# A paged-attention decoder step on one core: page numbers looked up once a turn by the sync engine

## The chip, the cores and the metric

The kernel runs on one core of a Trainium2 chip. The metric is the device time of one execution in microseconds (us); the median of several executions counts. Engines are called by their profile names: PE (TensorE matmul), PEld (its weight load), DVE (VectorE), ACT (ScalarE), POOL (GpSimd), SP (SyncE, which here only waits, looks up numbers and issues DMAs; its sequencer is SPq).

## What is computed

One step of a two-layer hybrid decoder. Layer A is a gated short convolution, layer B is forgetting attention with 16 heads of 64 over a shared set of keys and values, for 512 prompt tokens and for 8 sample sequences of 8 new tokens each. Each sample has 2048 past positions in 16 pages of 128 rows; which physical page holds which logical page stands in `page_table`:

```python
k_past = cache_k[page_table].reshape(nb, -1, N_HEADS, HEAD_DIM)
v_past = cache_v[page_table].reshape(nb, -1, N_HEADS, HEAD_DIM)
lf_past = cache_logf[page_table].reshape(nb, -1, N_HEADS).astype(jnp.float32)
k_all = jnp.concatenate([k_past, k_s.astype(k_past.dtype)], axis=1)
v_all = jnp.concatenate([v_past, v_s.astype(v_past.dtype)], axis=1)
F_all = jnp.cumsum(jnp.concatenate([lf_past, lf_s], axis=1), axis=1)
...
hs = _fox_layer(hs, sample_attend, b_norm[j], b_w_in[j], q_norm[j], b_w_out[j])
```

## The kernel before

It is written by hand: each engine has its own program, and semaphores join them. The order on an engine is the order of the code. Layer A and its output take the first 290 us. Then the queries of all heads are projected, and from about 377 us on there are eight turns (`heads(i)` on each engine, a hardware loop of seven turns and an unrolled last one).

Turn i does two things at once. It attends prompt head pair i, and it attends the past of sample i, for all 16 heads. The past needs 16 key pages and 16 value pages of 128 x 1024 numbers, 0.52 MB each. They pass through `page_ring`, 16 slots of 0.52 MB, which serves the keys first and the values after:

- Key slot n is loaded by two DMAs of 128 x 512 (0.26 MB, rows of 2 KB): slots 0 to 7 hold the first half of the heads' columns of all 16 pages, two pages a slot, slots 8 to 15 the second half. So each half looks up all 16 page numbers.
- DVE transposes each slot in place (line 1067), slots 0 to 3 at the end of the turn before, 4 to 7 and 8 to 15 in the turn itself.
- PE scores a half of the heads once eight slots are turned (`past_scores`, line 1450, 128 matmuls). Ahead of each half stands the last weight piece of a projection (line 1293), and PE waits in front of that piece for the eight transposes (`b_turned`).
- When half r is scored (`b_scored`), the value pages 8r to 8r + 7 may be loaded into its slots, one DMA of 128 x 1024 each (line 396).
- PE multiplies probabilities and values page by page (line 1557) between the prompt's steps; each step frees its slot (`b_used`), and the slot takes a key pair of the next sample.

SP issues nearly all DMAs in one queue. Its turn, in order: the prompt's log-forget sums (line 453), a weight slice of 0.52 MB (line 376), eight value pages, a weight slice, eight value pages, then the 16 key slots of the next sample, each behind `b_used`, with the suffix sums (1.05 MB, line 370) behind slot 8 and a weight slice behind slot 13, and the loop's branch (line 487). The other transfers of a turn are three stores of new keys and values, 0.56 MB, from ACT.

The page number comes from `page_of` (line 379): SP reads it from the SBUF tile `page_row` into a register, with a bounds check. Before each key slot there are two such lookups, before each value page one:

Of the kernel before, what the change touches and what calls it, by code (L numbers as in the profile page):

```python
# [31 lines left out]
P = 128  # L32
D = 1024
KT = D // P
SEQ = 512
NB = 8
NQ = 8
NS = NB * NQ
# [5 lines left out]
NPG = 16  # L44
# [3 lines left out]
NT = 5  # L48
# [4 lines left out]
HALF_D = D // 2  # L53
# [5 lines left out]
C_ID, C_ONESB, C_TRI, C_CM, C_NM, C_QD, C_RST, C_ONE = 0, 128, 256, 384, 512, 1024, 1088, 1152  # L59
# [18 lines left out]
def rows(t):  # L78
    return P if t < QB else NS
# [34 lines left out]
def build(nc, ctx, x_prompt, x_sample, state_conv, cache_k, cache_v, cache_logf, page_table,  # L114
# [9 lines left out]
    h_dram = nc.dram_tensor("h_scratch", [NT * P, D], F32, kind="Internal").ap()  # L124
# [4 lines left out]
    def place(name, shape, dt=F32, over=None):  # L129
        n = 4 if dt is not BF16 else 2  # L130
        for s in shape[1:]:
            n *= s
        n += (-n) % 32
        off = at["top"] if over is None else over
        if over is None:
            at["top"] += n
        at[name] = off
        return nc.alloc_sbuf_tensor_at(name, shape, dt, offset=off)
# [49 lines left out]
    def slot(n):  # L188
        return at["page_ring"] + n * 4 * D
# [5 lines left out]
    X2 = place("residual_b", [P, NT, D], over=slot(0))  # L195
# [27 lines left out]
    NBI = place("new_bias", [P, NB, NS], over=at["new_keys"] + 4 * NB * NS)  # L223
# [8 lines left out]
    def sem(name):  # L232
        return ctx.enter_context(nc.semaphore(name))
# [28 lines left out]
    b_used, b_qc, b_qt = sem("v_page_used"), sem("q_current_ready"), sem("q_pair_ready")  # L262
    b_turned, b_scored, b_taken = sem("k_pages_turned"), sem("past_scored"), sem("past_scores_taken")
    b_raw = [sem(f"b_w_loaded{s}") for s in range(2)]
    b_scaled, b_high, b_split, b_proj = sem("b_w_scaled"), sem("b_w_high"), sem("b_w_split"), sem("b_projected")
    b_dact, b_ddve = sem("proj_out_act"), sem("proj_out_dve")
    b_t0, b_t0f, b_t1, b_t1f = sem("turn0_full"), sem("turn0_free"), sem("turn1_full"), sem("turn1_free")
    b_c0, b_c0f, b_c1, b_c1f = sem("score0_full"), sem("score0_free"), sem("score1_full"), sem("score1_free")
    b_ss, b_ln, b_rr, b_normed = sem("head_squares"), sem("head_ln"), sem("head_rsqrt"), sem("head_normed")
    b_sfx, b_qz, b_nm = sem("suffix_loaded"), sem("q_spread_ready"), sem("new_mask_loaded")  # L270
# [13 lines left out]
    s_hld = sem("h_loaded")  # L284
# [9 lines left out]
    wo_b = b_w_out[0].rearrange("(k p) n -> p k n", p=P)  # L294
    kpages = cache_k.rearrange("g p h d -> g p (h d)")
    vpages = cache_v.rearrange("g p h d -> g p (h d)")
# [16 lines left out]
    def _(sp):  # L313
# [39 lines left out]
        def load_slab(w, col):  # L353
            sp.dma_start(WRA, w[:, :, bass.ds(col, SLAB)]).then_inc(l_raw, 16)
# [13 lines left out]
        def load_suffix(b):  # L368
            src = suffix_dram[bass.ds(b, 1), :, :].rearrange("a h n -> (a h) n")
            sp.dma_start(SS[:, :], src.unsqueeze(1).to_broadcast([H, NQ, PAST])).then_inc(b_sfx, 16)  # L370
# [4 lines left out]
        def load_w(w, col, slot):  # L375
            sp.dma_start(WR[:, slot, :, :], w[:, :, bass.ds(col, P)]).then_inc(b_raw[slot], 16)

        def page_of(b, n):
            return sp.value_load(PTAB[0:1, bass.ds(b * NPG + n, 1)], min_val=0, max_val=n_pool - 1)  # L379

        def load_keys(b, n, free=None):

            pages = [page_of(b, 2 * (n % 8) + e) for e in range(2)]
            if free:
                sp.wait_ge(*free)
            for e in range(2):
                src = kpages[bass.ds(pages[e], 1), :, n // 8 * HALF_D:(n // 8 + 1) * HALF_D]
                sp.dma_start(ring[:, n, e * HALF_D:(e + 1) * HALF_D],  # L388
                             src.rearrange("a p n -> (a p) n")).then_inc(b_page[n], 16)

        def load_values(b, n, free=None):
            page = page_of(b, n)
            if free:
                sp.wait_ge(*free)
            src = vpages[bass.ds(page, 1), :, :]
            sp.dma_start(ring[:, n, :], src.rearrange("a p n -> (a p) n")).then_inc(b_page[n], 16)  # L396

        sp.wait_ge(l_split, NSLAB)
# [4 lines left out]


        sp.wait_ge(s_rows, 16 * 9)
        sp.wait_ge(s_cs, H)
        for n in range(2):
            load_keys(0, n)
        for t in range(NT):
            sp.wait_ge(l_evac, 5 * (NSLAB - 1) + t + 1)  # L410
            sp.dma_start(h_dram[t * P:t * P + rows(t), :], X[0:rows(t), t, :]).then_inc(s_hst, 16)
        for n in range(2, 7):
            load_keys(0, n)
        sp.wait_ge(s_co, 1)
        sp.dma_start(conv_prompt[0, 0], CO[0:2, :]).then_inc(s_cost, 16)
        sp.dma_start(conv_sample[0].rearrange("b s n -> (b s) n"), CO[2:18, :]).then_inc(s_cost, 16)
# [3 lines left out]
        sp.wait_ge(s_hst, 16 * NT)  # L420
        sp.wait_ge(s_xl, 2 * NT)
        for n in range(7, 9):
            load_keys(0, n)

        sp.wait_ge(s_ft, 1)
        sp.dma_start(f_dram, FT[:, :]).then_inc(s_fst, 16)
# [5 lines left out]
        for n in range(4, KT + 3):  # L432
            sp.wait_ge(b_split, n - 1 if n < KT + 2 else n)
            if n < KT:
                load_w(wqz, n * P, n % 2)
            else:
                load_w(*((wkv, D), (wkv, 0), (wqz, KT * P))[n - KT], (0, 1, 1)[n - KT])
            if n < KT + 1:
                load_keys(0, 5 + n)
            if n == KT:  # L440

                sp.wait_ge(b_proj, 2)
                load_keys(0, 14)
                load_keys(0, 15)
        sp.wait_ge(s_fnr, 1)
        sp.dma_start(logf_prompt[0].rearrange("(t p) h -> p t h", p=P), LFN[:, 0:QB, :]).then_inc(s_out, 16)
        sp.dma_start(logf_sample.rearrange("b q h -> (b q) h"), LFN[0:NS, QB, :]).then_inc(s_out, 16)

        def heads(i, last):
            sp.wait_ge(b_c0f, 4 * i)  # L450
            sp.wait_ge(b_c1f, 4 * i)
            src = f_dram[bass.ds(2 * i, 2), 0:SEQ].unsqueeze(0).to_broadcast([P, 2, SEQ])
            sp.dma_start(FB[:, :, :], src).then_inc(b_fb, 16)
            if not last:
                sp.wait_ge(b_split, KT + 3 * i + 1)
                load_w(wkv, (i + 1 + KT) * P, 0)

            for n in range(NPG):
                load_values(i, n, (b_scored, 2 * i + n // 8 + 1) if n % 8 == 0 else None)
                if n == 7 and not last:  # L460
                    sp.wait_ge(b_split, KT + 3 * i + 3)
                    load_w(wkv, (i + 1) * P, 1)
            if last:
                sp.wait_ge(b_split, KT + 3 * NB)
                load_slab(wo_b, 0)

            for n in range(NPG):
                if last:
                    if n < NT:
                        sp.wait_ge(b_used, NPG * i + n + 1)  # L470
                        sp.dma_start(X2[0:rows(n), n, :], h_dram[n * P:n * P + rows(n), :]).then_inc(s_hld, 16)
                else:
                    load_keys(i + 1, n, (b_used, NPG * i + n + 1))
                if n == 8:

                    sp.wait_ge(b_t0, 8 * i + 4)
                    sp.wait_ge(b_t1, 8 * i + 4)
                    if last:
                        sp.dma_start(NBI[:, :, :].rearrange("p b n -> p (b n)"),
                                     table[:, C_NM:C_NM + NB * NS]).then_inc(b_nm, 16)  # L480
                    else:
                        load_suffix(i + 1)
                if n == 13 and not last:
                    sp.wait_ge(b_split, KT + 3 * i + 5)
                    load_w(wqz, (i + 1 + KT) * P, 1)

        with sp.Fori(0, NB - 1) as i:
            heads(i, False)
        heads(NB - 1, True)


        sp.wait_ge(b_t1f, 8 * NB)
# [1187 lines left out]
```

## Time and profile before

| | us |
|---|---|
| runs shown | 969.38, 959.49, 965.42; median 965.42 |
| profiled execution | 968.43 |
| its span | 966.6 |
| PE busy | 852.6 (88%) |
| DVE busy | 557.5 (58%) |
| ACT busy | 342.4 (35%) |
| POOL busy | 217.2 (22%) |
| mean DMA rate | 214 GB/s |

The profiled execution's own time is 1.8 us above its span. SP has no busy time in the profile, since it only issues; its instructions stand in the timeline and in the chain of work as SPq. Two ways of reading matter here. The timeline gives start and duration of merged instructions, and in brackets the idle time before them and what ended it. The chain in order of time lists pieces one after another; "issue" is time in which the engine waited for nothing that the profile shows.

### The profile page before, as it was taken

How to read it: one execution, taken by the hardware profiler on the slowest of the kernel's cores; microseconds unless marked ns; L12 is line 12 of the kernel's file. 1: busy time of each engine (PE TensorE's matmuls, PEld its weight loads, DVE VectorE, ACT ScalarE, POOL GpSimd, SP SyncE). 2: the span in 40 equal slices, each digit the busy share in tenths (PEclk: the TensorE clock that was granted, in tenths of full speed). 3: DMA queues.
4: the chain of work that ended last, by engine and by line, in shares of the span. 5: the costliest groups of instructions: out<-in, count | busy, mean ns of one | idle time of the engine just before them, and what ended most of it. 6: DMA issues, size and time to landing. Idle time of an engine off the chain costs nothing.

```text
span 966.6 us, 23640 instructions
## 1 busy us (share of the span) xinstructions
PE 852.6 (88%) x8516; PEld 707.5 (73%) x8516; DVE 557.5 (58%) x1039; ACT 342.4 (35%) x728; POOL 217.2 (22%) x130
## 2 busy tenths in 40 slices
PE   3899999999998997988787888887888878877998
PEld 2899999999997996756555656565556555654998
DVE  4745655555336355568485584684856746836632
ACT  4233333333025444252451442524514415235210
POOL 2233333331211032221322213203222132121000
PEclk8899999999999999899998998998999989989999
DMA  6232233323536463688998988998989889896212
GB/s 202 67 87 70 82 87 87 87 84 93 163 90 230 145 195 92 214 313 270 325 334 244 399 292 304 378 275 317 331 256 401 282 282 387 277 357 223 89 44 99
DMA packets 148482, 206.65 MB, mean 214 GB/s; under 512 B 10527, under 2 KB 93136, under 8 KB 147266
## 3 DMA queue, kind: packets, MB, share of 16 engines
q1 hardware_dynamic: 138802, 199.40, 61.6%
q10 hardware_dynamic: 9088, 4.46, 1.5%
q0 software_dynamic: 528, 2.10, 0.8%
q8 instruction: 20, 0.33, 0.1%
q14 instruction: 44, 0.36, 0.1%
HBM read 195.29 MB, written 10.63 MB: 213 GB/s over the span
## 4 chain that ended last, share of the span: by engine, by line
PE 54%; SPq 24%; issue 10%; DVE 7%; DMA 4%; ACT 1%; POOL 0%; DVEq 0%; ACTq 0%; POOLq 0%
PE psum L1293 31%; SPq L379 11%; PE psum L1319 9%; SPq L388 8%; PE psum L1450 4%; PE psum L1263 3%; SPq L396 2%; PE psum L1557 2%; DMA page_ring<-in_cache_k 2%; DVE page_ring L1067 1%; DMA w_raw<-in_a_w_in 1%; DMA w_raw<-in_a_w_out 1%; PE psum L1490 1%; PE psum L1512 1%; PE psum L1367 1%
## 5 line engine op out<-in xcount | busy, mean ns | idle before, releaser
L1293 PE MATMUL psum<-xn_high,w_high 128*128 128x256 f32 x992 | 230.4, 314 | 45.2 <-DVE page_ring L1067 42.3
L1293 PEld LDWEIGHTS psum<-xn_high,w_high 128*128 128x128 f32 x992 | 167.8, 193 | 79.3 <-DVE page_ring L1067 45.8
L1293 PE MATMUL psum<-xn_low,w_high 128*128 128x256 f32 x992 | 216.0, 300 | 0.0
L1293 PE MATMUL psum<-xn_high,w_low 128*128 128x256 f32 x992 | 215.5, 299 | 0.0
L1067 DVE STREAM_TRANSPOSE page_ring<-page_ring 128x1024 f32<-128x1024 f32 x128 | 153.4, 1224 | 32.8 <-DMA page_ring<-in_cache_k 31.2
L1293 PEld LDWEIGHTS psum<-xn_low,w_high 128*128 128x128 f32 x992 | 170.5, 193 | 0.0
L1293 PEld LDWEIGHTS psum<-xn_high,w_low 128*128 128x128 f32 x992 | 170.4, 193 | 0.0
L551 POOL TENSOR_TENSOR w_raw<-w_raw,gains 128x1024 f32<-128x1024 f32 x32 | 61.6, 1927 | 275.3 <-DMA w_raw<-in_b_w_in 244.0
L913 DVE TENSOR_TENSOR w_low<-w_raw,w_high 128x1024 fp32r<-128x1024 f32 x32 | 54.1, 1692 | 74.5 <-ACT w_high L629 74.5
L1450 PE MATMUL psum<-page_ring,q_current 32*32 32x512 f32 x2048 | 84.1, 700 | 0.0
L528 POOL TENSOR_TENSOR w_raw<-w_raw,gains 128x1024 f32<-128x1024 f32 x30 | 60.8, 2027 | 89.6 <-DMA w_raw<-in_a_w_in 89.6
L560 POOL TENSOR_TENSOR w_low<-w_raw,w_high 128x1024 fp32r<-128x1024 f32 x22 | 52.1, 2368 | 124.4 <-ACT w_high L680 124.4
L1557 PE MATMUL psum<-page_ring,p_turned 128*32 128x256 f32 x1024 | 75.2, 388 | 0.0
L629 ACT ACTIVATE w_high<-w_raw 128x1024 fp32r<-128x1024 f32 x32 | 33.9, 1060 | 94.8 <-PE psum L1293 67.7
L680 ACT ACTIVATE w_high<-w_raw 128x1024 fp32r<-128x1024 f32 x30 | 31.7, 1055 | 90.2 <-POOL w_raw L551 81.2
L1450 PEld LDWEIGHTS psum<-page_ring,q_current 32*32 32x32 f32 x2048 | 36.9, 112 | 36.0 <-issue 28.6
L1095 DVE COPY ks_t<-k_t 128x64 f32 (+1 forms) x8 | 2.2, 271 | 63.3 <-PE psum L1450 63.3
L1557 PEld LDWEIGHTS psum<-page_ring,p_turned 128*32 128x32 f32 x1024 | 23.4, 108 | 20.8 <-issue 13.6
L731 ACT ACTIVATE q_current<-queries 32x64 f32 (+1 forms) x128 | 32.5, 254 | 3.9 <-DVE queries L1044 1.0
L1080 DVE COPY probs_t<-psum 128x512 f32<-128x512 f32 (+3 forms) x32 | 15.4, 482 | 26.6 <-PE psum L1263 26.4
L796 ACT ACTIVATE probs<-probs,tiny 128x512 f32<-128x512 f32 (+1 forms) x32 | 19.3, 605 | 24.5 <-DVE tiny L1129 23.4
L1263 PE MATMUL psum<-constants,sample_scores 128*128 128x128 f32 x128 | 18.6, 278 | 10.6 <-DVE p_turned L1080 8.6
(243 smaller groups left out, 1429.8 us busy)
## 6 DMA issues: line engine op xcount, KB each, us to landing
page_ring<-in_cache_k SPq DMA_DIRECT2D x256, 256.0 KB, 4.1
page_ring<-in_cache_v SPq DMA_DIRECT2D x128, 512.0 KB, 6.5
w_raw<-in_a_w_in SPq DMA_DIRECT2D x32, 512.0 KB, 4.0
sample_scores<-suffix_scratch SPq DMA_DIRECT2D x8, 1024.0 KB, 9.6
w_raw<-in_b_w_in SPq DMA_DIRECT2D x16, 512.0 KB, 5.1
w_raw<-in_kv_w SPq DMA_DIRECT2D x16, 512.0 KB, 5.9
w_raw<-in_a_w_out SPq DMA_DIRECT2D x4, 1024.0 KB, 4.9
f_broad<-f_scratch SPq DMA_DIRECT2D x8, 512.0 KB, 4.1
```

Of the source, the lines that this page charges most:

```text
L379: return sp.value_load(PTAB[0:1, bass.ds(b * NPG + n, 1)], min_val=0, max_val=n_pool - 1)
L388: sp.dma_start(ring[:, n, e * HALF_D:(e + 1) * HALF_D], src.rearrange("a p n -> (a p) n")).then_inc(b_page[n], 16)
L528: pool.tensor_tensor(WR[:, q % 2, :, :], WR[:, q % 2, :, :], gain(G_A), ALU.mult).then_inc(a_scaled, 1)
L551: pool.tensor_tensor(WR[:, slot, :, :], WR[:, slot, :, :], gain(g), ALU.mult).then_inc(b_scaled, 1)
L560: pool.tensor_tensor(WL[:, slot, :, :], WR[:, slot, :, :], WH[:, slot, :, :].bitcast(F32), ALU.subtract).then_inc(b_split, 1)
L913: dve.tensor_tensor(WL[:, slot, :, :], WR[:, slot, :, :], WH[:, slot, :, :].bitcast(F32), ALU.subtract).then_inc(a_split, 1)
L1067: dve.transpose(ring[:, n, :], ring[:, n, :]).then_inc(b_turned, 1)
L1263: return pe.transpose(out, src, CT[0:r, C_ID:C_ID + r])
L1293: mm = pe.matmul(PS[:, bank + h, 0:c.stop - c.start], w[:, k, :], x[:, k, c], start=(k == 0 and n == 0), stop=(k == KT - 1 and n == 2))
L1319: mm = pe.matmul(PS[0:r, bank, 0:SLAB], x[:, k, toks(t)], wp[:, k, :], start=(k == 0 and p == 0), stop=(k == KT - 1 and p == 2))
L1450: mm = pe.matmul(PS[32 * j:32 * j + 32, T0 + g, :].rearrange("p (n k) -> p n k", k=32), QC[32 * g:32 * g + 32, j, 64 * h + 32 * a:64 * h + ...
L1557: mm = pe.matmul(PS[32 * j:32 * j + 32, OS, 0:4 * HD].rearrange("p (a n) -> p a n", a=2), PTS[:, k, 32 * j:32 * j + 32], ring[:, k, :].rea ...
```

## The change

The 16 page numbers of a sample are looked up in one block and stay in registers for both key halves and for the values. For sample 0 the block stands ahead of its first key load; for the others at the head of `next_turn`. For that the loop is cut at another place: a turn of the loop on SP is now the keys of sample i + 1 followed by its values (and the DMAs between them), where it was the values of sample i followed by the keys of sample i + 1. The last turn's loads are written out behind the loop, and its new mask (`new_bias`) is issued behind the five reloads of the residual. The other engines' programs are the same.

```diff
-        def load_keys(b, n, free=None):
-
-            pages = [page_of(b, 2 * (n % 8) + e) for e in range(2)]
+        def load_keys(pages, n, free=None):
+
             if free:
                 sp.wait_ge(*free)
             for e in range(2):
-                src = kpages[bass.ds(pages[e], 1), :, n // 8 * HALF_D:(n // 8 + 1) * HALF_D]
+                src = kpages[bass.ds(pages[2 * (n % 8) + e], 1), :, n // 8 * HALF_D:(n // 8 + 1) * HALF_D]
...
-        def load_values(b, n, free=None):
-            page = page_of(b, n)
-            if free:
-                sp.wait_ge(*free)
-            src = vpages[bass.ds(page, 1), :, :]
+        def load_values(pages, n):
+            src = vpages[bass.ds(pages[n], 1), :, :]
             sp.dma_start(ring[:, n, :], src.rearrange("a p n -> (a p) n")).then_inc(b_page[n], 16)
...
         sp.wait_ge(s_rows, 16 * 9)
+
+        first = [page_of(0, n) for n in range(NPG)]
         sp.wait_ge(s_cs, H)
...
-        def heads(i, last):
+        def values(pages, i, last):
...
             for n in range(NPG):
-                load_values(i, n, (b_scored, 2 * i + n // 8 + 1) if n % 8 == 0 else None)
+                if n % 8 == 0:
+                    sp.wait_ge(b_scored, 2 * i + n // 8 + 1)
+                load_values(pages, n)
...
+        def next_turn(i, last):
+
+            pages = [page_of(i + 1, n) for n in range(NPG)]
             for n in range(NPG):
...
+                load_keys(pages, n, (b_used, NPG * i + n + 1))
                 if n == 8:
 
                     sp.wait_ge(b_t0, 8 * i + 4)
                     sp.wait_ge(b_t1, 8 * i + 4)
...
+                    load_suffix(i + 1)
+                if n == 13:
                     sp.wait_ge(b_split, KT + 3 * i + 5)
                     load_w(wqz, (i + 1 + KT) * P, 1)
-
-        with sp.Fori(0, NB - 1) as i:
-            heads(i, False)
-        heads(NB - 1, True)
+            values(pages, i + 1, last)
+
+        values(first, 0, False)
+        with sp.Fori(0, NB - 2) as i:
+            next_turn(i, False)
+        next_turn(NB - 2, True)
+        sp.wait_ge(b_split, KT + 3 * NB)
+        load_slab(wo_b, 0)
+        for t in range(NT):
+            sp.wait_ge(b_used, NPG * (NB - 1) + t + 1)
+            sp.dma_start(X2[0:rows(t), t, :], h_dram[t * P:t * P + rows(t), :]).then_inc(s_hld, 16)
```

What this makes of SP's queue shows in the order of the built program. In the loop, one key slot of the kernel before (`page_ring<-in_cache_k` are the key DMAs, TENSOR_LOAD the lookup, ISA and REGISTER_ALU register arithmetic, checks and waits):

```order
L379 ISA
L379 TENSOR_LOAD page_row
L379 ISA x3
L379 TENSOR_LOAD page_row
L379 ISA x2
L388 ISA
L388 DMA page_ring<-in_cache_k 128x512
L388 ISA
L388 DMA page_ring<-in_cache_k 128x512
```

The same slot in the changed kernel:

```order
L384 REGISTER_ALU
L387 ISA
L387 DMA page_ring<-in_cache_k 128x512
L387 ISA
L387 DMA page_ring<-in_cache_k 128x512
```

The two lookups are gone from the slot; the two DMAs and what computes their addresses are left. The second place is the end of the loop, on SP: before, the last key slot and the branch.

```order
L379 TENSOR_LOAD page_row
L379 ISA x2
L379 TENSOR_LOAD page_row
L379 ISA x2
L385 REGISTER_ALU
L388 ISA
L388 DMA page_ring<-in_cache_k 128x512
L388 ISA
L388 DMA page_ring<-in_cache_k 128x512
L487 REGISTER_ALU
L487 COMPARE_AND_BRANCH
```

In the changed kernel the loop ends with the second eight value pages (`page_ring<-in_cache_v`):

```order
L461 REGISTER_ALU
L376 ISA
L376 DMA w_raw<-in_kv_w 128x8x128
L458 REGISTER_ALU
L392 DMA page_ring<-in_cache_v 128x1024 x8
L480 REGISTER_ALU
L480 COMPARE_AND_BRANCH
```

The branch moved from behind the keys to behind the values, and the eight value DMAs stand in a row with no instruction between them. The loop begins with the 16 lookups, then come the keys.

## Rows read from the trace of the kernel before

**Rows 1.** The page, chain that ended last, shares of the span by line.

```profile
PE psum L1293 31%; SPq L379 11%; PE psum L1319 9%; SPq L388 8%; PE psum L1450 4%; PE psum L1263 3%; SPq L396 2%; PE psum L1557 2%; DMA page_ring<-in_cache_k 2%; DVE page_ring L1067 1%; DMA w_raw<-in_a_w_in 1%; DMA w_raw<-in_a_w_out 1%; PE psum L1490 1%; PE psum L1512 1%; PE psum L1367 1%
```

**Rows 2.** Timeline of SP, one turn: start, duration in us, merged issues.

```profile
526.65 0.40 SPq L453 DMA_DIRECT2D f_broad<-f_scratch  x1
...
528.73 9.05 SPq L396 DMA_DIRECT2D page_ring<-in_cache_v  x8
...
539.38 8.58 SPq L396 DMA_DIRECT2D page_ring<-in_cache_v  x8
549.44 19.82 SPq L388 DMA_DIRECT2D page_ring<-in_cache_k  x18
...
571.60 10.00 SPq L388 DMA_DIRECT2D page_ring<-in_cache_k  x10
...
583.52 3.11 SPq L388 DMA_DIRECT2D page_ring<-in_cache_k  x4
```

**Rows 3.** The chain in order of time, pieces of three turns: start, us, what.

```profile
586.81 3.50 issue
...
779.39 5.52 DMA page_ring<-in_cache_k
...
828.92 0.27 SPq L379
...
829.47 0.27 SPq L379
...
830.22 0.34 SPq L388
...
830.76 0.33 SPq L388
```

**Rows 4.** Timeline of PE, weight pieces, scores, last value step; idle before in brackets.

```profile
386.46 0.85 PE L1293 MATMUL psum<-xn_high,w_high 128*128 128x256 f32 x2 [4.00 <-DVE page_ring L1067]
...
446.88 0.53 PE L1293 MATMUL psum<-xn_high,w_high 128*128 128x256 f32 x2 [1.22 <-DVE page_ring L1067]
...
447.87 4.46 PE L1450 MATMUL psum<-page_ring,q_current 32*32 32x512 f32 x128
...
526.75 0.85 PE L1293 MATMUL psum<-xn_high,w_high 128*128 128x256 f32 x2 [4.25 <-DVE page_ring L1067]
...
528.50 6.14 PE L1450 MATMUL psum<-page_ring,q_current 32*32 32x512 f32 x128
...
567.26 0.64 PE L1557 MATMUL psum<-page_ring,p_turned 128*32 128x256 f32 x8
...
591.06 0.85 PE L1293 MATMUL psum<-xn_high,w_high 128*128 128x256 f32 x2 [3.80 <-DVE page_ring L1067]
```

**Rows 5.** The page, costliest groups: count, busy, mean ns, idle before and its releaser.

```profile
L1293 PE MATMUL psum<-xn_high,w_high 128*128 128x256 f32 x992 | 230.4, 314 | 45.2 <-DVE page_ring L1067 42.3
```

**Rows 6.** Busy time of the score matmuls alone (line 1450), turns 1 to 7.

```profile
440.00:862.00 422.00, 73.42 (x1792) 32.25 (x1792) 0.95 0.92 318
```

**Rows 7.** Timeline of DVE, transposes of turn 0 and turn 3.

```profile
377.28 9.13 DVE L1067 STREAM_TRANSPOSE page_ring<-page_ring 128x1024 f32<-128x1024 f32 x8
...
576.88 1.23 DVE L1067 STREAM_TRANSPOSE page_ring<-page_ring 128x1024 f32<-128x1024 f32 x1
```

**Rows 8.** Stretches, PE PEld DVE ACT POOL busy; last three: PE clock, DMA share, GB/s.

```profile
526.75:591.20 64.45, 54.91 (x655) 38.10 (x655) 41.46 (x84) 23.97 (x64) 14.04 (x9) 0.95 0.92 319
...
725.00:727.50 2.50, 2.50 (x67) 1.40 (x37) 0.47 (x1) 0.00 (x0) 1.61 (x1) 1.00 1.04 417
...
755.00:757.50 2.50, 1.57 (x24) 0.57 (x16) 2.46 (x3) 1.14 (x2) 1.86 (x1) 1.00 0.68 240
...
765.00:767.50 2.50, 1.55 (x12) 1.31 (x10) 2.50 (x3) 0.00 (x0) 0.00 (x0) 1.00 1.06 228
```

**Rows 9.** Timeline of SP, the last three key slots of sample 0.

```profile
354.98 5.24 SPq L388 DMA_DIRECT2D page_ring<-in_cache_k  x6
```

More of the change, by code:

```diff
@@ L405, in _ @@
         sp.wait_ge(s_rows, 16 * 9)
+        first = [page_of(0, n) for n in range(NPG)]
         sp.wait_ge(s_cs, H)
         for n in range(2):
-            load_keys(0, n)
+            load_keys(first, n)
         for t in range(NT):
@@ L412, in _ @@
         for n in range(2, 7):
-            load_keys(0, n)
+            load_keys(first, n)
         sp.wait_ge(s_co, 1)
@@ L422, in _ @@
         for n in range(7, 9):
-            load_keys(0, n)
+            load_keys(first, n)
         sp.wait_ge(s_ft, 1)
@@ L438, in _ @@
             if n < KT + 1:
-                load_keys(0, 5 + n)
+                load_keys(first, 5 + n)
             if n == KT:
                 sp.wait_ge(b_proj, 2)
-                load_keys(0, 14)
-                load_keys(0, 15)
+                load_keys(first, 14)
+                load_keys(first, 15)
         sp.wait_ge(s_fnr, 1)
@@ L462, in heads @@
                     load_w(wkv, (i + 1) * P, 1)
-            if last:
-                sp.wait_ge(b_split, KT + 3 * NB)
-                load_slab(wo_b, 0)
+        def next_turn(i, last):
+            pages = [page_of(i + 1, n) for n in range(NPG)]
             for n in range(NPG):
[L468 to L473, printed above, removed]
+                load_keys(pages, n, (b_used, NPG * i + n + 1))
                 if n == 8:
@@ L477, in heads @@
                     sp.wait_ge(b_t1, 8 * i + 4)
[L478 to L483, printed above, removed]
+                    load_suffix(i + 1)
+                if n == 13:
                     sp.wait_ge(b_split, KT + 3 * i + 5)
                     load_w(wqz, (i + 1 + KT) * P, 1)
-        with sp.Fori(0, NB - 1) as i:
-            heads(i, False)
-        heads(NB - 1, True)
+            values(pages, i + 1, last)
[8 more added lines that the diff above has]
+            sp.dma_start(X2[0:rows(t), t, :], h_dram[t * P:t * P + rows(t), :]).then_inc(s_hld, 16)
+        sp.wait_ge(b_t0, 8 * (NB - 1) + 4)
+        sp.wait_ge(b_t1, 8 * (NB - 1) + 4)
+        sp.dma_start(NBI[:, :, :].rearrange("p b n -> p (b n)"), table[:, C_NM:C_NM + NB * NS]).then_inc(b_nm, 16)
         sp.wait_ge(b_t1f, 8 * NB)
```

## The prediction

> **What bounds the kernel now.** I read the chain that ended last first, then the queue of the sync engine (SP) over one turn, then what TensorE (PE) waits for, then the DMA rates. The chain [rows 1] puts SP's sequencer on the path: 11% of the span on the lookup, line 379, and 8% on the key issues, line 388. That is unusual for an engine that computes nothing, and the turn shows why [rows 2]: SP issues the scratch row of log-forget sums at 526.65, eight value pages from 528.73 and eight from 539.38, then keys from 549.44 to 586.63 (583.52 + 3.11), and after that the next turn begins. Nothing in that row of issues is a long wait; SP is simply busy from end to end. The first eight value pages take 9.05 us, 1.2 us each; a key slot takes about 2.3 us (from 571.60, four slots and a last pair of issues in 10.00 us).
>
> The price of a part [rows 3]: the two lookups ahead of a key slot start at 828.92 and 829.47, so 0.55 us each; the two key issues start at 830.22 and 830.76, so 0.54 us each. Half of a key slot is lookup. After the last key of a turn the sequencer stands for 3.50 us at the loop's branch (586.81 in rows 3).
>
> What comes late through this is the last key. In one turn it was issued at 779.39 and landed 5.52 us later [rows 3]. VectorE (DVE) turns it at once, and PE waits for that: 4.25 us at 526.75, 3.80 us at 591.06 [rows 4]. The page's group for the weight pieces shows 42.3 us of such waits [rows 5]; there are 15 of them, two in each turn but the first. Turn 0's is 4.00 us, at 386.46, behind eight transposes in a row. Seven are the waits of 1.22 us for the first half of the keys (446.88 shows one): there DVE is the engine that is behind, with four transposes back to back. So 42.3 - 4.00 - 7 x 1.22 = 29.8 us are the seven waits for the second half, in turns 1 to 7.
>
> The wait costs a second time. After it PE's clock stands at the lower level: the half's score matmuls, 4.46 us at 447.87, take 6.14 us at 528.50 [rows 4], and over all fourteen halves of turns 1 to 7 they are busy 73.42 us [rows 6], 73.42 - 14 x 4.46 = 11.0 us too much. The weight piece ahead takes 0.99 us when warm (446.88 to 447.87) and 1.75 us when cold (526.75 to 528.50); I count it cold in six of the seven turns: 6 x 0.76 = 4.6 us.
>
> **The change, part by part.** Let T0 be the moment at which PE could start the weight piece ahead of the second half, in a turn in which it didn't wait. The turn from 526.75 gives the rest of the times. PE's next T0 is its end of work ahead of the wait at 591.06, 591.06 - 3.80 = 587.26, less 526.75, less the cold clock's 2.44: T0 + 58.1. DVE begins the second half's transposes at 576.88, T0 + 47.7, and eight without a gap take 9.13 us, at 377.28 [rows 7]: T0 + 56.8. So both allow a turn of 58.1 us where it takes 64.45 [rows 8], if the last key has landed by T0 + 56.8, one transpose ahead.
>
> Lookups: 48 a turn (16 for values, 32 for keys) become 16. 32 x 0.55 = 17.6 us of SP's time go. The 16 that stay now stand in a block ahead of the first key. Key issues stay, 2 x 0.54 us and 0.1 us for the wait a slot: 16 x 1.2 = 19 us. A value issue loses its lookup and its address arithmetic: one instruction and its move, about 0.45 us. The loop's branch moves from behind the keys to behind the values. I take it at what it costs now, 3.50 us and 0.8 us of arithmetic round it; bounds are 0 and twice that.
>
> When is the first key issued? The second half's scores are done at T0 + 0.99 + 4.46 = T0 + 5.5. Then eight values, 3.6; branch, 4.3; 16 lookups, 8.8: T0 + 22.2. In the turn now it is 549.44 - 526.75 = 22.7 after the cold start, T0 + 20.3. The first key thus starts 1.9 us later. What hides it: the DMA engines are still busy with values then (below). The last key is issued after 19 us and 1.1 for suffix sums and weights: T0 + 42. The value step that frees its slot ends at 567.26 + 0.64 = 567.90 [rows 4], T0 + 38.7. Today the last issue is at T0 + 57.4. So it is issued 15 us sooner, and no wait for a free slot comes in its place.
>
> What is late next is the transfer. A turn moves 319 GB/s x 64.45 us = 20.6 MB [rows 8]. With a backlog the rate is 417 GB/s, and where only SP's pace feeds the keys it is 240 at 0.68 busy. At 410 GB/s the turn's bytes are 50 us. The suffix sums are slower (228 GB/s at full share at 765 in rows 8): 1.05 MB, 2.0 us more. If the 2.1 MB of weights and log-forget sums, also in short rows, went as slowly, 4.1 us more: 50 to 56 us of work in a turn of 58.1. The keys: 16 slots of 0.52 MB, 8.4 MB, at 410 are 20.5, suffix 4.6, one weight piece 1.3 to 2.3; from T0 + 22.2 done by T0 + 49 to 50, and landed by T0 + 55 even if all the 5.52 us of rows 3 come on top. Ahead of them, values 0 to 7 are issued at T0 + 51 of the turn before and values 8 to 15 at T0 + 5.5; with the sums, weights and stores that is 10.5 MB, drained near T0 + 17 to 20. The order fits, with 2 to 4 us to spare on the last key, and with none if every part is slow.
>
> The Trainium skill ("DMA: Bandwidth & Descriptors", Specifications) gives about 358 GB/s as a core's limit at HBM. By that rule alone 20.6 MB would take 57.5 us, and the turn would have no slack. The row at 417 GB/s [rows 8] speaks against it here.
>
> "Advanced Engine Details and Errata" of the Trainium skill (Control Flow Timing) has a compare-and-branch at some 108 ns; this trace has 3.50 us behind one [rows 3], and the measurement decides. By the page the first key would go out 3.4 us sooner; the sum would be the same, the slack larger.
>
> Other edits. At the start 14 lookups more stand ahead of the first key issue: 7.7 us. The stores of the residual behind it are waited for by evacuations anyway, each later key slot becomes 1.1 us cheaper, and the last keys go out by 360.22 while DVE turns the first at 377.28 [rows 7, 9]. Nothing, bounds 0 to +2 us. In the last turn the values go out earlier and the mask stands a little later in the queue; nothing, bounds -1 to +1 us, since PE's value steps aren't waiting for pages.
>
> The sum: 29.8 + 11.0 + 4.6 = 45.4 us, against the profiled execution's 968.4: 923. That execution was 3.0 us above the median of the runs shown, 965.4, so **920 us** for a median.
>
> **The rivals.** (B) The DMA engines become the bound. They are busy 0.92 of the turn, 59.3 us [rows 8]; if that is work that can't be packed closer, and they stand 1 to 3 us between the last value and the first key, a turn takes 60.3 to 62.3, some 3.2 us less than 64.45. 7 x 3.2 = 22 us: 968.4 - 22 - 3 = 943 us, or 940 where the cold clock goes in part. For it: the high share. Against it: the share reads 1.04 with a backlog, and at 0.68 it carries only 240 GB/s, so it isn't a measure of work. A queue that holds SP back once eight values are in it would have the same effect: the first key late by the backlog it may not queue, 3 to 9 us.
>
> (C) No change: SP's issues aren't what delays the last key, its transfer is, so it lands at the same time. Against it: SP feeds the keys at 240 GB/s where the engines have shown 417, so nothing queues ahead of the last one for long. 960 to 968 us.
>
> (D) Slower: key transfers of 2 KB rows can't run faster than the 240 GB/s that they show at 755 [rows 8], whatever SP does. Then they take 35 us and the suffix sums, as now, but begin behind a block of 16 lookups and the branch: 22.2 + 2.4 (the cold clock stays) against 22.7, 1.9 us later each turn, 7 x 1.9 = 13 us: 979 us. It decides if the rate stays under 250 with keys alone queued. Against it: the DMA share is 0.68 at that rate.
>
> That the registers don't hold the pages (a reload at every use) can be excluded: the order has no load between issues.
>
> **How the numbers follow.** Forecast 0.64, B 0.25, C 0.06, D 0.05. About 1% either way is what a measurement of this kernel can tell from none. The forecast and B are both faster by over 1%, so 0.89; same 0.06; slower 0.05. The forecast's own range is 912 (the runs differ by some 5 us either way, and the branch may cost less) to 930 (a residual wait of 1.5 us a turn). Reaching to B gives 912 to 943.
>
> **What would show it.** The chain has almost no SP left in the turns; waits of PE on the transposes fall from 42.3 us to about 13 us, the score matmuls' 73.42 us to 63 us; turns are 58 us apart; the DMA rate in a turn is 350 GB/s; SP waits for the value steps and the scores. Wrong would be: DVE waits for key transfers late in the turn with the DMA share near 1 (B), SP's value issues growing well beyond 0.45 us (a full queue), or keys alone at 240 GB/s (D).

## The result, and the profile after

The changed kernel takes 925.29 us, the median of four runs (924.18 to 928.07), against 962.45 us for four runs of the kernel before beside it. The ratio is 0.9612, 95% interval 0.9543 to 0.9681: faster by 3.2 to 4.6%. The forecast was 920 us, the likeliest case, with a range of 912 to 943.

The profiled execution took 924.18 us (span 922.4), where the one before took 968.43. The page of the kernel after: engine totals, the clock by slice, one line of the DMA queues, then the chain by engine and by line, then two of the costliest groups. Line 388 has become 387, 396 has become 392, the loop's branch is line 480, and the lines of the other engines are one higher than before.

```profile
PE 837.3 (91%) x8516; PEld 701.5 (76%) x8516; DVE 545.6 (59%) x1039; ACT 342.4 (37%) x728; POOL 217.3 (24%) x130
...
PEclk9999999999999999899999999999999999998999
...
q14 instruction: 13, 0.11, 0.0%
...
PE 68%; DVE 14%; SPq 7%; issue 5%; DMA 4%; ACT 1%; DVEq 0%; POOL 0%; ACTq 0%; POOLq 0%
PE psum L1294 37%; PE psum L1320 10%; PE psum L1451 7%; DVE page_ring L1068 5%; SPq L387 4%; PE psum L1264 4%; PE psum L1558 3%; DMA page_ring<-in_cache_k 2%; PE psum L1491 1%; PE psum L1513 1%; DVE probs_odd L1138 1%; DMA w_raw<-in_a_w_in 1%; DMA w_raw<-in_a_w_out 1%; DVE tiny L1129 1%; DVE probs L1124 1%
...
L1294 PE MATMUL psum<-xn_high,w_high 128*128 128x256 f32 x992 | 226.8, 310 | 19.8 <-DVE page_ring L1068 16.9
...
L1068 DVE STREAM_TRANSPOSE page_ring<-page_ring 128x1024 f32<-128x1024 f32 x128 | 149.5, 1215 | 6.2 <-DMA page_ring<-in_cache_k 5.6
```

The lookup (line 379), the second largest line of the chain in [rows 1], is gone from the first fifteen. The key issues have 4% left of 8%, and what SP gave up PE and DVE have taken. PE's waits for the transposes are 16.9 us against 42.3 in [rows 5]. The line of queue q14 will matter below: its transfers are of kind instruction, and the kernel before had 44 of them:

```profile
q14 instruction: 44, 0.36, 0.1%
```

The timeline of PE after, the rows that answer to [rows 4]; idle before in brackets. The first is turn 0's first half, the last the second half of turn 3.

```profile
385.54 6.51 PE L1451 MATMUL psum<-page_ring,q_current 32*32 32x512 f32 x128
...
399.65 4.46 PE L1451 MATMUL psum<-page_ring,q_current 32*32 32x512 f32 x128
...
446.16 0.53 PE L1294 MATMUL psum<-xn_high,w_high 128*128 128x256 f32 x2 [1.22 <-DVE page_ring L1068]
...
459.22 4.46 PE L1451 MATMUL psum<-page_ring,q_current 32*32 32x512 f32 x128
...
517.87 0.53 PE L1294 MATMUL psum<-xn_high,w_high 128*128 128x256 f32 x2 [1.55 <-DVE page_ring L1068]
...
577.23 0.53 PE L1294 MATMUL psum<-xn_high,w_high 128*128 128x256 f32 x2 [1.31 <-DVE page_ring L1068]
```

The waits of 4.25 and 3.80 us in [rows 4] have become 1.55 and 1.31 us, and only in turns 2 and 3: the other five second halves start at once. The sum checks: 5.51 us ahead of turn 0, 7 x 1.22 for the first halves, 1.55 and 1.31 make 16.9. The score matmuls of the second half take 4.46 us again. Their busy time in turns 1 to 7, to be held against 73.42 in [rows 6] (columns as there):

```profile
440.00:862.00 422.00, 62.49 (x1792) 29.34 (x1792) 0.99 0.99 337
```

The turns, each from one second half's scores to the next; columns as in [rows 8]:

```profile
399.65:459.22 59.57, 53.51 (x656) 37.67 (x655) 41.19 (x84) 24.51 (x64) 11.14 (x6) 0.97 0.95 313
459.22:518.86 59.64, 52.31 (x656) 36.80 (x655) 41.17 (x84) 24.50 (x64) 14.59 (x9) 1.00 1.02 342
518.86:578.22 59.36, 52.31 (x656) 36.80 (x655) 40.99 (x84) 24.50 (x64) 14.70 (x9) 1.00 1.03 345
578.22:636.02 57.80, 52.04 (x655) 36.77 (x654) 40.64 (x84) 24.50 (x64) 15.76 (x10) 1.00 1.04 358
...
693.82:751.62 57.80, 52.05 (x656) 36.76 (x655) 40.87 (x84) 24.51 (x64) 13.45 (x8) 1.00 1.02 348
```

Three turns take 59.4 to 59.6 us and four take 57.8 to 57.9 (the two not shown 57.80 and 57.87), where [rows 8] has 64.45. PE's clock is at full level from the second of them on.

SP in the turn that ends at the third of those rows (timeline; start, duration, merged issues), to be read beside [rows 2]:

```profile
511.63 6.31 SPq L392 DMA_DIRECT2D page_ring<-in_cache_v  x8
...
523.35 6.58 SPq L392 DMA_DIRECT2D page_ring<-in_cache_v  x8
541.42 10.19 SPq L387 DMA_DIRECT2D page_ring<-in_cache_k  x18
...
552.80 7.22 SPq L387 DMA_DIRECT2D page_ring<-in_cache_k  x10
...
561.32 7.89 SPq L387 DMA_DIRECT2D page_ring<-in_cache_k  x4
```

And the chain of the same turn in order of time, at the loop's branch and at the last key slot:

```profile
530.09 0.26 issue
530.35 0.07 SPq L480
530.42 0.04 issue
530.47 0.30 SPq L379
...
561.32 5.27 SPq L387
...
568.88 7.03 DMA page_ring<-in_cache_k
```

Three things in these rows were not in the forecast. The 3.50 us behind the branch [rows 3] have shrunk to some 0.4. The last four key DMAs need 7.89 us to be issued, because one issue instruction alone stands for 5.27 us; in [rows 2] the last four need 3.11 with two lookups among them. And the last key is issued at 568.88 and lands 7.03 us later, not 5.52. The issue instruction of 5.27 us has no semaphore to wait for, so it is taken here to stand in front of a full DMA queue; the kernel with halved keys below bears that out. So the time that the lookups and the branch set free is partly spent there.

### The profile page after: what moved, and what is told of

Same layout as the page of the kernel before. It is cut to its first block, busy times and chain, and to the rows that moved or that the text cites. A ratio compares the mean times of both kernels' runs of the same rounds, so it can differ in the third digit from the quotient of the medians.

```text
span 922.4 us, 22692 instructions
## 1 busy us (share of the span) xinstructions
PE 837.3 (91%) x8516; PEld 701.5 (76%) x8516; DVE 545.6 (59%) x1039; ACT 342.4 (37%) x728; POOL 217.3 (24%) x130
## 3 DMA queue, kind: packets, MB, share of 16 engines
q10 hardware_dynamic: 9088, 4.46, 1.6%
## 4 chain that ended last, share of the span: by engine, by line
PE 68%; DVE 14%; SPq 7%; issue 5%; DMA 4%; ACT 1%; DVEq 0%; POOL 0%; ACTq 0%; POOLq 0%
PE psum L1294 37%; PE psum L1320 10%; PE psum L1451 7%; DVE page_ring L1068 5%; SPq L387 4%; PE psum L1264 4%; PE psum L1558 3%; DMA page_ring<-in_cache_k 2%; PE psum L1491 1%; PE psum L1513 1%; DVE probs_odd L1138 1%; DMA w_raw<-in_a_w_in 1%; DMA w_raw<-in_a_w_out 1%; DVE tiny L1129 1%; DVE probs L1124 1%
## 5 line engine op out<-in xcount | busy, mean ns | idle before, releaser
L1294 PE MATMUL psum<-xn_high,w_high 128*128 128x256 f32 x992 | 226.8, 310 | 19.8 <-DVE page_ring L1068 16.9
L1294 PE MATMUL psum<-xn_low,w_high 128*128 128x256 f32 x992 | 213.6, 297 | 0.0
L1294 PEld LDWEIGHTS psum<-xn_high,w_high 128*128 128x128 f32 x992 | 165.8, 191 | 52.8 <-issue 29.6
L1294 PEld LDWEIGHTS psum<-xn_high,w_low 128*128 128x128 f32 x992 | 168.2, 190 | 0.0
L1294 PEld LDWEIGHTS psum<-xn_low,w_high 128*128 128x128 f32 x992 | 168.1, 190 | 0.0
L1068 DVE STREAM_TRANSPOSE page_ring<-page_ring 128x1024 f32<-128x1024 f32 x128 | 149.5, 1215 | 6.2 <-DMA page_ring<-in_cache_k 5.6
L914 DVE TENSOR_TENSOR w_low<-w_raw,w_high 128x1024 fp32r<-128x1024 f32 x32 | 50.4, 1576 | 77.4 <-ACT w_high L630 77.4
L1451 PE MATMUL psum<-page_ring,q_current 32*32 32x512 f32 x2048 | 73.5, 614 | 0.0
L1451 PEld LDWEIGHTS psum<-page_ring,q_current 32*32 32x32 f32 x2048 | 34.2, 104 | 27.4 <-issue 18.1
L1264 PE MATMUL psum<-constants,sample_scores 128*128 128x128 f32 x128 | 18.6, 278 | 10.6 <-DVE p_turned L1081 8.6
```

Of the source, the lines that this page charges most:

```text
L914: dve.tensor_tensor(WL[:, slot, :, :], WR[:, slot, :, :], WH[:, slot, :, :].bitcast(F32), ALU.subtract).then_inc(a_split, 1)
L1068: dve.transpose(ring[:, n, :], ring[:, n, :]).then_inc(b_turned, 1)
L1264: return pe.transpose(out, src, CT[0:r, C_ID:C_ID + r])
L1294: mm = pe.matmul(PS[:, bank + h, 0:c.stop - c.start], w[:, k, :], x[:, k, c], start=(k == 0 and n == 0), stop=(k == KT - 1 and n == 2))
L1451: mm = pe.matmul(PS[32 * j:32 * j + 32, T0 + g, :].rearrange("p (n k) -> p n k", k=32), QC[32 * g:32 * g + 32, j, 64 * h + 32 * a:64 * h + ...
```

## The experiments

Eleven kernels ran in three groups, each beside the kernel before; its medians in the groups were 967.37, 966.01 and 967.12 us. The changed kernel itself was not run again in them; its 925.29 us stands beside 962.45. The question was twofold: whether SP's time was what held the turns back, as forecast (theory S), or the transfers; and what the branch had to do with it, since its stall had gone unasked.

### The kernel before with SP's loop written out

```diff
-        with sp.Fori(0, NB - 1) as i:
+        for i in range(NB - 1):
```

> The kernel before with SP's loop of seven turns written out, so without its branch; all lookups stay. Theory S (SP's queue, full from end to end, sets the turn of the kernel before): the 4.0 to 5.4 us between a turn's last key issue and the next turn go, so the turn falls from 64.5 to about 60.2 us, 7 x 4.3 = 30 us, plus some of the cold clock: 930 to 940 us. Rival L (the lookups alone are what counts): within 1% of before, 955 to 967 us.

It took 933.83 us (933.01 to 938.99), ratio 0.967 (0.9617 to 0.9723). That is S's range (930 to 940), and rival L's (955 to 967) is excluded. All 48 lookups are still there, and most of the gain is made without touching them. The group of the weight pieces on its page:

```profile
L1293 PE MATMUL psum<-xn_high,w_high 128*128 128x256 f32 x992 | 228.1, 312 | 27.5 <-DVE page_ring L1067 24.0
```

24.0 us of waits, 18 less than in [rows 5], and turns of about 60 us. SP's time was the bound, and 4 us a turn off it, or 17 us off it, go most of the same way: the turns can fall only from 64.5 us to what PE and DVE need.

### The new queue order alone, lookups as before

```diff
-        def load_keys(pages, n, free=None):
+        def load_keys(b, n, free=None):
+            pages = [page_of(b, 2 * (n % 8) + e) for e in range(2)]
...
-        def load_values(pages, n):
+        def load_values(b, n, free=None):
+            page = page_of(b, n)
```

The label is "rotated": the changed kernel's loop, cut between values and keys, with a lookup at each use.

> The changed kernel's order of loop and turns, with the old lookups at each use (48 a turn). Theory S: SP has the same work as before, only in another order: within 1% of before, 953 to 972 us. Rival R (the place of the branch and of the first key make the gain, not the lookups): near the changed kernel, 925 to 935 us.

It took 985.9 us (985.34 to 993.28), ratio 1.0219 (1.0159 to 1.028). That is slower than the kernel before, outside what S expected (953 to 972), and far from the rival's 925 to 935. The page's group and SP's timeline around the branch:

```profile
L1296 PE MATMUL psum<-xn_high,w_high 128*128 128x256 f32 x992 | 230.3, 314 | 61.5 <-DVE page_ring L1070 58.5
```

```profile
609.56 9.79 SPq L396 DMA_DIRECT2D page_ring<-in_cache_v  x8
627.24 7.63 SPq L388 DMA_DIRECT2D page_ring<-in_cache_k  x7
```

From the end of the value issues, 609.56 + 9.79 = 619.35, to the first key issue at 627.24 pass 7.9 us, with only two lookups in them. So the stall exists in this order as well: in the trace 5.5 to 6.1 us pass from the branch to the next instruction, at each of the five backward branches, where the six of the kernel before have 3.5 to 5.3. The same kernel with SP's loop written out separates the stall from the order:

```diff
-        with sp.Fori(0, NB - 2) as i:
+        for i in range(NB - 2):
```

> The queue order of the changed kernel with the lookups at each use (48 a turn), and SP's loop written out instead of a hardware loop. Theory S (what made the same kernel with a loop 985.9 us is the stall at SP's branch, some 4 us on the path of each turn, and what follows from it; the order itself costs little): 930 to 945 us, like the kernel before with its loop written out (933.8), and no gap over 1 us between a turn's last value issue and the next lookup. Rival R (the order keys-then-values itself costs the time, since the lookups then stand at worse places): 965 to 990.

It took 932.91 us (928.83 to 937.7), ratio 0.9638 (0.9598 to 0.9677), with 24.3 us of waits. SP's timeline at the same place:

```profile
585.86 11.12 SPq L396 DMA_DIRECT2D page_ring<-in_cache_v  x8
598.28 18.57 SPq L388 DMA_DIRECT2D page_ring<-in_cache_k  x18
```

1.3 us instead of 7.9, and the time is that of the kernel before written out (933.83), as S expected. The order of the queue costs nothing that these runs can tell; the hardware loop cost the 53 us. In the two profiled executions the difference is 47.6 us of span (983.4 against 935.8): the five stalls together are 28.7 us, and PE is busy 12.5 us longer with the same work (854.6 against 842.1) at a lower clock (mean 0.948 against 0.983), behind waits of 7.4 to 9.8 us before the second half of turns 2 to 6. The other 6 us are not accounted for.

### What makes the stall come and go

The written-out loops show that the stall belongs to the hardware loop, but the changed kernel has such a loop too, and no stall. The length of the loop body differs: from branch to branch the trace has 346 instructions of SP in the kernel before and in "rotated", and 234 in the changed kernel (these counts include a MOVE ahead of each DMA, which the order doesn't list). The changed kernel with unused lookups at the head of each turn (8, 16, 28 of them) changes both SP's time and the body's length:

```diff
+            for n in range(28):
+                page_of(i, n)
             pages = [page_of(i + 1, n) for n in range(NPG)]
```

> The changed kernel with 8 lookups more, unused, at the head of each next turn (24 instead of 16), for turns 1 to 7. They put the first key off by 8 x 0.64 = 5.1 us. Theory T (the transfers have next to no slack left, 0 to 1.5 us): the last key lands 4 to 5 us later in each turn, 7 x 4 = 28 us and part of the cold clock: 948 to 965 us. Rival H (2 to 4 us of slack, as the prediction had it): 7 x 1 to 3 us, 930 to 946 us. If the loop's branch gets its stall back with the longer loop, both come out 4 us a turn higher.

> The same with 16 lookups more (32 instead of 16), 10.2 us ahead of the first key. Theory T: 9 us a turn and the cold clock of all seven, 2.4 us each: 925 + 7 x 11.4 = 1005 us, 990 to 1010. Rival H: 975 to 990 us. A stall at the branch behind the values would add 4 us a turn and show as a gap behind it.

> The changed kernel with 28 unused lookups at the head of each turn, which make SP's loop body as long as that of the kernel before, 291 instructions. The 12 lookups more than in the kernel with 16 extra (992.9 us) are 12 x 0.66 x 7 = 55 us. Theory L (the stall comes with a long loop body): the stall of some 3.5 us is back at the five backward branches, 1062 to 1075 us, and the trace shows 3 to 4 us between SP's branch and the next instruction. Rival O (the stall belongs to what stands ahead of the branch, key issues before and value issues now, or to their order, and not to the length): 1040 to 1052 us and a gap under 0.5 us.

| extra lookups | SP's instructions, branch to branch | median us | ratio to before | from branch to next instruction |
|---|---|---|---|---|
| 0 | 234 | 925.29 | 0.9612 (0.9543 to 0.9681) | 0.26 to 0.29 us |
| 8 | 259 | 957.88 | 0.9885 (0.9818 to 0.9951) | 0.24 to 0.29 us |
| 16 | 283 | 992.88 | 1.027 (1.0205 to 1.0336) | 0.24 to 0.29 us |
| 28 | 330 | 1076.8 | 1.1144 (1.1105 to 1.1184) | 5.7 to 6.0 us |

The instruction totals of the pages agree: 22866, 23034 and 23352 are 174, 342 and 660 more than the changed kernel's 22692, over seven turns. A lookup thus adds 3.1 to 3.4 instructions on average, and 28 of them don't make the body as long as that of the kernel before, as their expectation has it, but leave it 16 instructions shorter.

The chain of the kernel with 16 extra, and of the one with 28:

```profile
615.37 0.04 SPq L482
615.42 0.24 issue
615.66 0.06 SPq L482
```

```profile
568.18 0.06 SPq L482
568.24 5.81 issue
574.05 0.07 SPq L482
```

With 330 instructions the stall is back, at all five backward branches, and the time has it: 992.88 + 12 x 0.66 x 7 = 1048 for the lookups alone, and 5 x 5.8 = 29 more is 1077. Theory L holds in kind, with a longer stall than its 3 to 4 us and a time 2 us above its 1062 to 1075; O, which needed 1052 or less and no gap, falls: the same value issues stand ahead of the branch with 16 extra lookups and with 28. The DMA queue of the instructions agrees; its line on the page of either:

```profile
q14 instruction: 14, 0.11, 0.0%
```

```profile
q14 instruction: 40, 0.33, 0.1%
```

These packets come while SP stands: of the kernel with 28 extra, two in each of the stretches 568.2 to 574.1 and 650.6 to 656.5 and three more in the rest of the turn; of the kernel with 16 extra, none between 478 and 621, a stretch with three branches. So at each turn of a long body instructions are fetched anew, and SP stands until they are there. "Runtime: NRT & Kernel Launch" of the Trainium skill (Instruction fetch mechanics) describes it: instructions come in blocks of 256, two of which an engine holds, and a taken branch to a block that it no longer holds waits for a fetch. The trace agrees in kind. The lengths alone don't settle it: 330 is less than two such blocks hold, so by that account the body would have to lie across three of them. Where the limit lies between 283 and 330, and whether the place of the body in the stream counts beside its length, no run shows.

The kernels with 8 and 16 extra also say something of the slack of the changed kernel; both times lie where theory T had them (948 to 965, 990 to 1010). A lookup in a block takes 0.66 us there (24 of them and the branch lie between 606.79 and 623.30), so 8 add 5.3 us to a turn, 37 us to seven. The time grew by 32.6. That alone would leave 0.6 us of slack a turn. But PE was busy 14.0 us longer there with the same work (851.3 against 837.3), the clock again, and 32.6 - 14.0 = 18.6 us would leave 2.6. So the slack, as an estimate, is 0.6 to 2.6 us a turn, and in turns 2 and 3 of the changed kernel there is none. The next 8 cost 35.0, of which 11.1 are PE's longer busy time.

### Keys halved: is it the transfer?

In both kernels the key DMAs of samples 1 to 7 move 256 of their 512 columns:

```diff
+            w = HALF_D // 2 if free else HALF_D
...
-                src = kpages[bass.ds(pages[e], 1), :, n // 8 * HALF_D:(n // 8 + 1) * HALF_D]
-                sp.dma_start(ring[:, n, e * HALF_D:(e + 1) * HALF_D],
+                src = kpages[bass.ds(pages[e], 1), :, n // 8 * HALF_D:n // 8 * HALF_D + w]
+                sp.dma_start(ring[:, n, e * HALF_D:e * HALF_D + w],
```

The kernel before:

> The kernel before, but for samples 1 to 7 each key DMA moves only half its columns (256 of 512), so half of the past keys aren't loaded; SP's instructions are as many. Theory S: the last key is late because it is issued late; half the bytes save at most 1 us of its landing: 950 to 965 us, waits of PE on the transposes still over 30 us. Rival C (the transfer is the bound before): waits fall under 20 us and the time to 925 to 935 us.

956.96 us (955.58 to 959.15), ratio 0.9898 (0.985 to 0.9946). Its group of the weight pieces:

```profile
L1294 PE MATMUL psum<-xn_high,w_high 128*128 128x256 f32 x992 | 228.0, 312 | 40.8 <-DVE page_ring L1068 37.4 <-DVE xn_low L900 2.6 <-DVE w_low L998 0.9
```

With 4.2 MB of a turn's 20.6 gone the waits are still 37.4 us. What was late in the kernel before was the issue, and only a little the transfer: the time is inside S's 950 to 965, and C's 925 to 935 is excluded.

The changed kernel:

> The changed kernel with the same halved key DMAs for samples 1 to 7. Theory S with PE and DVE as the bound of the turn after: the two waits of 1.3 to 1.6 us in turns 2 and 3 go, the rest stays: 0 to 4 us under the changed kernel, 921 to 926 us, turns of 57.8 us. Rival B (the DMA engines are the bound after): turns get shorter by 2 us or more, under 912 us.

921.83 us (917.56 to 925.92), ratio 0.9517 (0.9468 to 0.9565). The same group:

```profile
L1295 PE MATMUL psum<-xn_high,w_high 128*128 128x256 f32 x992 | 227.5, 312 | 15.4 <-DVE page_ring L1069 12.5 <-DVE xn_low L901 2.0 <-DVE w_low L999 0.9
```

The second-half waits are gone and all turns take 57.9 to 58.2 us, yet the median falls by 3.5 us only, and the two intervals overlap. Rival B needed less than 912: the DMA engines aren't the bound of the changed kernel either, they only use up its slack. The long issue instructions shrink with the bytes: the longest for a key takes 2.73 us where the changed kernel has 6.35, and the last four key DMAs of a turn are issued in 2.6 to 2.8 us where they took 7.89. SP's program is the same, so it is the backlog of transfers that holds an issue.

### Lookups off the path, and without any

In the changed kernel with SP's loop written out the 16 lookups of the next sample can stand elsewhere: behind the values, or ahead of the wait for the second half's scores, where SP stands anyway.

```diff
+                if n == 8:
+                    ahead = None if last else [page_of(i + 1, m) for m in range(NPG)]
                 if n % 8 == 0:
                     sp.wait_ge(b_scored, 2 * i + n // 8 + 1)
...
+        pages = values(first, 0, False)
+        for i in range(NB - 1):
+            pages = next_turn(pages, i, i == NB - 2)
```

> The changed kernel with SP's loop written out. Its branch costs 0.1 us in the trace, so theory T: no change, 921 to 929 us. Rival F (the straight program has to be fetched all the way, and that costs what the loop saves): over 932 us.

> The changed kernel written out, with the 16 lookups of the next sample ahead of the wait for the second half's scores, where SP stands anyway; the first key goes out some 10 us sooner. Theory T: the DMA queue never runs dry between values and keys, the waits of turns 2 and 3 (1.55 and 1.31 us) go: 919 to 925 us, turns at 57.8 us, set by PE and DVE. Rival B (the DMA engines, 1.03 busy, are the bound of the turn): no gain beyond the straight program's, and some wait stays.

Behind the values 918.87 us (916.91 to 924.91), ratio 0.9496 (0.9437 to 0.9555); ahead of the wait 923.47 (919.94 to 924.89), ratio 0.9537 (0.9474 to 0.9601). The two overlap. By the medians they are 0.7% and 0.2% below the changed kernel, by the ratios 1.2% and 0.8%, with intervals that overlap its own. The first lies 2 us below T's 921 to 929, the second in its 919 to 925, and rival F (over 932) falls. Of second-half waits the traces keep 1.19 and 1.06 us in the first and 0.76 us in the second. The last run has no lookups at all, in the order of the kernel before, and constant pages, the same 16 for all samples, in place of those of the table:

```diff
-            return sp.value_load(PTAB[0:1, bass.ds(b * NPG + n, 1)], min_val=0, max_val=n_pool - 1)
+            return 9 * n % n_pool
```

> The kernel before with constant page numbers (9n modulo the pool's size, the same 16 for all samples) and no lookup at all, so the keys and values attended are not those of the page table. It is the kernel before without lookups and, with a short loop body, without the stall, in its own queue order. Theory T (SP's time alone holds the turns back; with none of it left PE and DVE set them): 916 to 926 us, no waits for the second half's transposes in the steady turns. Rival Q (DMA work, or the order of the queue, holds turns at 60 us or more whatever SP does): 930 to 943.

917.99 us (914.75 to 922.04), ratio 0.9486 (0.9439 to 0.9533): T's 916 to 926, not Q's 930 to 943. One turn of it, columns as in [rows 8]:

```profile
519.05:576.85 57.80, 52.04 (x656) 36.76 (x655) 40.62 (x84) 24.50 (x64) 15.13 (x9) 1.00 1.04 357
```

57.80 us, the same as the fast turns of the changed kernel, at the same DMA rate, and no second-half wait is left. That is what PE and DVE need, and some 918 us is the floor as far as these kernels show, however cheap SP becomes. The changed kernel is 7 us above it by the medians, 12 by the ratios (0.9612 against 0.9486); in its trace the seven turns together are 5.2 us above seven of 57.80.

## Why the prediction came out right

The likeliest case was the true one: SP held the turns back, and they fell to what PE and DVE allow. The number, 920, is 5.3 us (0.6%) below the measured 925.3. Point by point:

- **The second-half waits, 29.8 us.** 1.55 + 1.31 = 2.9 us are left of them. The remaining waits (4.00, now 5.51, and 7 x 1.22) stayed. That 5.51 isn't the change's doing as far as can be seen: the kernel before written out, whose start is the old one, has 5.52 there too.
- **The cold clock, 11.0 + 4.6 us.** The score matmuls of turns 1 to 7 fell from 73.42 to 62.49 us, 10.9. The weight piece takes 0.99 us in turn 2 even behind its wait (517.87 to 518.86), as warm.
- **The turn, 58.1 us allowed.** 57.8 to 57.9 in four turns, 57.80 in the run without lookups. Three turns took 59.4 to 59.6; above 57.80 all seven are 5.2 us too long. Two of them hold the waits left. The first shows a clock of 0.97: from 420.65 to 423.65 it was granted at 0.53, close to the lower level, behind a stretch (417.65 to 420.65) in which PE was busy for 1.49 of 3.00 us. Why it fell in this turn and in no other isn't settled.
- **The sum against the profiled execution, 45.4 us.** It lost 44.3, but not all where the sum had it. From the second half's scores of turn 0 (402.01 before, 399.65 after) to those of turn 7 the time is 450.88 before and 409.84 after: 41.0 us. The start gave 2.4 and the end 0.8. The start is chance: the first 286 us, in code that the change doesn't touch, ran 4.1 us sooner, at a higher granted clock, and 1.5 of that went to the longer wait ahead of turn 0.
- **The slack of 2 to 4 us.** The working of this step failed. The last key was forecast to be issued at T0 + 42 and landed by T0 + 55, with T0 + 56.8 as the limit. In the turn whose rows stand above, T0 is 517.87 - 1.55 = 516.32; the last key is issued at 568.88, T0 + 52.6, and landed at 575.91, T0 + 59.6. The steps in it: first key T0 + 25.1, not 22.2 (1.55 of the difference is the wait itself); eight values 6.58 us, not 3.6, of which the first stands for 3.19 alone; 16 lookups 10.95, not 8.8, since most in the block take 0.64 us each where the pairs between key issues take 0.55; keys 27.4 us from first to last, not 20, 5 to 6 of it in a single issue. In the next two turns, which end without a wait, the last key is still issued at T0 + 49.9 and T0 + 48.0. The halved keys remove that backlog, and the waits go; the extra lookups put the mean slack at 0.6 to 2.6 us (estimate above).
- **The branch, kept at 3.50 + 0.8 us.** This failed the other way: the stall vanished with the shorter loop body, and 0.5 us pass from the last value issue to the first lookup (529.93 to 530.47). From the kernel with 8 extra lookups, which has 5.3 us a turn more on the path and takes 957.9, a stall of 3.5 to 5.8 us at the five backward branches would have cost some 15 to 26 us (at the same 32.6 us for 37): an estimate of 940 to 951 us, at the upper end of the forecast's range of 912 to 943 or beyond it, and far from its 920. The forecast's bound for the branch, "0 and twice that", held both ends, but the sum didn't follow either of them through, and the place where the branch moved to (from beside a wait for the scores to the path between the last value and the first key) was costed as hidden. "Rotated" shows that there it is not.

So two mis-sized terms, SP's issues too cheap and the branch too dear, worked against each other. In the turn of the rows the steps ahead of the last key took 14.4 us more than forecast and the branch 3.8 less; so the last key was issued 10.6 us later than forecast. The forecast had left it 14.8 us between issue and limit; with 7.0 us to land it came 2.8 us past the limit, which is the 1.55 us of the wait before and the 1.31 us of the wait that follows. That the total of the whole kernel came within 0.6% is in part luck: nothing in the forecast said that the shorter body would take the stall away.

- **Rivals.** B had its mechanism, a queue that holds SP back, but not its price: at most the 7 to 12 us above the floor, not 20. Its sentence on "SP's value issues growing well beyond 0.45 us" came true without deciding the time. C falls with the halved keys of the kernel before. D falls with the rate: it needed less than 250 GB/s with keys alone queued, and from 604 to 607, between a turn's first key issue and its suffix sums, the stretch reads 321 (columns as in [rows 8]), and those beside it 218 (602 to 604) and 376 (607 to 610):

```profile
604.00:607.00 3.00, 3.00 (x39) 1.58 (x36) 1.19 (x5) 1.79 (x7) 0.00 (x0) 1.00 0.88 321
```

How the gain divides between fewer lookups and the shorter body depends on which comes first, for the two are not additive. Without its stall but with all lookups, the kernel before gains 33.5 us (967.37 to 933.83). Where no loop stalls, fewer lookups in the order of the change are worth 14 us (932.91 to 918.87, different groups). So most of what the forecast put down to the 32 lookups that go can be had by taking the stall alone. What the lookups would bring with the stall kept at its old length no run shows. In the order that the change needs, the lookups are what makes the difference of 986 to 925, stall included.

## What to carry to other kernels

An engine that only issues DMAs can be the bound; read its queue over one turn as one reads a compute engine, lookup by lookup, and look for the gap at its loop's branch. When the other engines set a floor close by, several unequal savings buy the same time, so cost each against the floor. And when a loop is cut at another place, follow the branch to where it now stands: what a wait covered before may lie on the path, unless the body has become short enough to keep.

## What the hardware showed

- A hardware loop on SP stood behind its branch for 3.5 to 5.3 us in the kernel before (3.82 at 457.82, 3.50 at 586.81), for 5.5 to 6.1 us in "rotated" (346 instructions from branch to branch in both) and for 5.7 to 6.0 us in the kernel with 28 extra lookups (330), and for 0.24 to 0.29 us with 234 to 283. The packets of instruction transfers tell the loops apart on the page: 44, 41 and 40 against 13 and 14. The kernels with SP's loop written out have 20 and 28, and no branch to stand at.
- A DMA issue normally takes SP 0.33 to 0.39 us. Behind a backlog it took up to 6.35 us for a key, with no semaphore to wait for, and 3.19 us for the first value of a half, counted from the end of the scores that it waits for.
- In turns 2 to 7 of the changed kernel the rate is 342 to 363 GB/s at a DMA share of 1.02 to 1.05. A fifth less to move (the halved keys) brought its median down by 3.5 us only, so a share of 1.0 is not by itself a sign that the DMA engines are the bound.
